# V rows gathered by token and summed on TensorE in four column quarters, h for the U dot products in PSUM

## The reference, cut to what matters

```python
q = (hf @ w_q).astype(f32).reshape(t, PEER_HEADS, 2, PEER_HALF)
...
s1, i1 = lax.top_k(scores[:, :, 0], PEER_TOPK)
s2, i2 = lax.top_k(scores[:, :, 1], PEER_TOPK)
...
idx = (e1 * N_KEYS + e2).reshape(t, PEER_HEADS * PEER_TOPK)
gates = jax.nn.softmax(top_s, axis=-1).reshape(t, PEER_HEADS * PEER_TOPK)
...
def block(args):
    hb, ib, gb = args
    act = jax.nn.gelu(jnp.einsum('td,tkd->tk', hb, u_tab[ib]).astype(f32), approximate=False)
    return jnp.einsum('tk,tkd->td', (gb * act).astype(hb.dtype), v_tab[ib])
```

## Time and profile before

| | us |
|---|---|
| median of three executions | 3935.57 |
| lowest, highest | 3903.57, 3950.37 |
| profiled execution, span from the first to the last instruction | 3815.1 |
| busy in it: TensorE matmul | 2493.9 |
| VectorE (DVE) | 2729.9 |
| ScalarE (ACT) | 552.7 |
| GpSimd (POOL) | 2477.6 |

### The profile page before, as it was taken

The page is one execution under the profiler, slowest core; times in us unless marked ns, Lnnn a source line. Parts: engine busy times, 40 slices in busy tenths (PEclk is TensorE's granted clock), DMA queues, the critical chain, the costliest instruction groups (busy, mean ns, idle before and its releaser), DMA issues. The chain is left out here.

```text
span 3815.1 us, 28982 instructions
## 1 busy us (share of the span) xinstructions
PE 2493.9 (65%) x7042; PEld 1238.9 (32%) x7042; DVE 2729.9 (72%) x5120; ACT 552.7 (14%) x1065; POOL 2477.6 (65%) x2125
## 2 busy tenths in 40 slices
PE   7999863566677667666766666566666667654166
PEld 4444452422243324322433233323332343211022
DVE  3332045989788878887788778787888788867844
ACT  2221010101111111111111111111111111111011
POOL 1100000687777778777787877787778777877776
PEclk9999986788787778788877888788878788877588
DMA  3334400899899999999999899999999999999998
GB/s 100 110 105 149 163 8 14 299 335 372 328 353 365 349 334 334 361 356 334 344 350 359 318 345 353 343 339 342 356 374 345 341 364 376 346 341 391 369 367 323
DMA packets 349585, 1159.17 MB, mean 304 GB/s; under 512 B 41216, under 2 KB 70800, under 8 KB 348432
## 3 DMA queue, kind: packets, MB, share of 16 engines
q0 software_dynamic: 301024, 1094.89, 78.0%
q1 hardware_dynamic: 46256, 58.69, 4.5%
q10 hardware_dynamic: 2176, 4.35, 0.3%
HBM read 1128.37 MB, written 29.43 MB: 303 GB/s over the span
## 5 line engine op out<-in xcount | busy, mean ns | idle before, releaser
L811 PE MATMUL y_psum<-ring,diag 128*128 128x512 f32 x1984 | 1216.2, 751 | 981.1 <-DMA ring<-in_peer_v_dram,at_row 669.6
L1136 DVE CUSTOM_DVE_ANT_0 ring<-ring,h_e 128x1024 f32<-128x1024 f32 x1024 | 1243.9, 1223 | 377.3 <-DMA ring<-in_peer_u_dram,at_row 367.2
L791 POOL DMA_INDIRECT ring<-in_peer_u_dram,at_row x986 | 1182.0, 1199 | 331.5 <-issue 278.9
L791 POOL DMA_INDIRECT ring<-in_peer_v_dram,at_row x704 | 835.3, 1187 | 217.2 <-issue 196.3
L811 PEld LDWEIGHTS y_psum<-ring,diag 128*128 128x128 f32 x1984 | 418.2, 231 | 1677.9 <-issue 878.0
L1158 DVE SCALAR_TENSOR_TENSOR y<-ring,coef,y 128x1024 f32<-128x1024 f32 x528 | 678.9, 1286 | 207.2 <-DMA ring<-in_peer_v_dram,at_tail 116.5
L791 POOL DMA_INDIRECT ring<-in_peer_v_dram,at_tail x320 | 366.0, 1144 | 119.1 <-issue 94.5
L995 ACT ACTIVATE diag<-ident_m,coef 128x128 f32<-128x128 f32 x496 | 190.6, 399 | 1130.1 <-PE y_psum L811 1014.3
L315 PE MATMUL proj<-hn_T,w_blk 128*128 128x512 f32 x640 | 280.0, 596 | 1.3 <-DVE hn_T L444 1.3
L944 PE MATMUL tile_psum<-w_q,arena 128*128 128x512 f32 x512 | 245.1, 641 | 8.8 <-ACT arena L1076 8.8
L775 POOL COPY at_head<-picks 128x10 uint32<-128x10 uint32 x8 | 4.2, 530 | 313.9 <-DVE picks L1377 312.6
...
...
## 6 DMA issues: line engine op xcount, KB each, us to landing
ring<-in_peer_u_dram,at_row POOLq DMA_INDIRECT x986, 6.3
ring<-in_peer_v_dram,at_row POOLq DMA_INDIRECT x704, 6.3
...
ring<-in_peer_v_dram,at_tail POOLq DMA_INDIRECT x320, 6.3
```

The costliest lines, as they stand in the source:

```text
L791: pool.indirect_dma_start(ring[:, j], None, tables[kind], bass.IndirectOffsetOnAxis(ap=at, axis=0)).then_inc(filled[j], 16)
L811: last = nc.tensor.matmul(y_ps[:, half], diag[:, k % 2], ring[:, slot_of(item, e), half * BANK:(half + 1) * BANK], start=(k == 0), stop=(n ...
L1136: nc.vector.tensor_tensor_reduce(out=ring[:, j], in0=ring[:, j], in1=h2_e[:], scale=1.0, scalar=0.0, op0=ALU.mult, op1=ALU.add, accum_out= ...
```

## The change

- A V gather brings, for one token, the V rows of its 128 picks, one per partition. For this the matrix of picks is turned: TensorE turns `top_id`, DVE copies it to `picks_T`, POOL copies that to `at_T`; a gather's offsets are one column of it. U gathers read `picks` itself.
- The sum over a token's picks is then the sum over partitions. TensorE does it with a weight matrix of 128 picks x 32 columns in which only the token's column is not zero. Four tokens, one of each quarter of the tile, form a group: their outputs are the four quarters of partitions of `y_ps`, so a group is 2 halves x 4 quarters of matmuls 128x32 by 128x512. `spread` holds these weight matrices, written by DVE in blocks of four groups (item "E"), each block once the block two before is used.
- No V sum is left on DVE, no diagonal on ScalarE; `PACE`, `split_v`, `GROUP` are gone. Gelu and gate product are done once for all 128 picks behind the last U; `coef` is turned by TensorE into `y_ps` and copied to `coef_T`.
- The order: first the 80 V of the tile before (20 groups), with 64 U mixed in, then 64 U, then gelu, then the first 48 V (12 groups). `MARKS` lays 26 shares over the first part up to "X", 14 up to "G", the rest over the V at the end, which fall beside the top-k.
- h for the U dot products is in PSUM (`h_ps`, two banks). The mixer's PSUM `bank` shrinks from six to four banks: its steps use other banks, the state products of SSD move behind the solve, and `S_gdn_ready` is waited for ahead of the output projection.
- SP waits for `picks_T_ready` instead of `picks_ready` before it loads the next tile's mixer data. `spread` is zeroed once at the start.

The core of the diff (the renumbered banks of the mixer and of ScalarE's copies are left out):

```diff
 
 
 SLOTS = 10
-GROUP = 32
-LAG = 40
-TAIL = PICKS - LAG
-HEAD = SLOTS
-assert LAG % SLOTS == 0
+QUADS = 4
+STEPS = P // QUADS
+BLOCK_STEPS = 4
+BLOCKS_E = STEPS // BLOCK_STEPS
+FRONT_STEPS = 12
+FRONT = FRONT_STEPS * QUADS
+BACK = P - FRONT
+MIXED_U = 64
+PITCH = 33
+assert BACK % SLOTS == 0
 
 
 def expert_sequence():
-    seq, v = [], 0
-    for n in range(PICKS):
-        seq.append(("U", n, 0))
-        while v < min(LAG, (n + 1) * 4 // 3 + 1):
-            seq.append(("V", TAIL + v, 1))
-            v += 1
-        if n >= LAG:
-            seq.append(("V", n - LAG, 0))
-        if n % GROUP == GROUP - 1:
-            seq.append(("G", n // GROUP, 0))
-        if n == 3:
-            seq.append(("C", PICKS // GROUP - 1, 1))
-        if n % GROUP == 5 and n > GROUP:
-            seq.append(("C", n // GROUP - 1, 0))
-        for at, item in ((8, ("K", 0, 0)), (30, ("F", 0, 1)), (33, ("O", 0, 1)), (LAG - 1, ("X", 0, 0))):
-            if n == at:
-                seq.append(item)
+
+
+    seq, n = [], 0
+    back_steps = STEPS - FRONT_STEPS
+    for g in range(back_steps):
+        i = FRONT_STEPS + g
+        seq += [("V", QUADS * i + q, 1) for q in range(QUADS)]
+        if g % BLOCK_STEPS == 1 and i // BLOCK_STEPS + 1 < BLOCKS_E:
+            seq.append(("E", i // BLOCK_STEPS + 1, 1))
+        to = MIXED_U * (g + 1) // back_steps
+        seq += [("U", k, 0) for k in range(n, to)]
+        n = to
+    for k in range(n, P):
+        if k == n + 4:
+            seq.append(("F", 0, 1))
+        if k == n + 7:
+            seq.append(("O", 0, 1))
+        if k == n + 16:
+            seq.append(("X", 0, 0))
+        seq.append(("U", k, 0))
+    seq += [("G", 0, 0), ("C", 0, 0), ("E", 0, 0), ("E", 1, 0)]
+    for i in range(FRONT_STEPS):
+        seq += [("V", QUADS * i + q, 0) for q in range(QUADS)]
+        if i % BLOCK_STEPS == 1 and i >= BLOCK_STEPS:
+            seq.append(("E", i // BLOCK_STEPS + 1, 0))
     return seq
 
...
+    ends = []
+    for (a, at), (b, to) in zip(MARKS, MARKS[1:]):
+        ends += [at + round((to - at) * (n - a) / (b - a)) for n in range(a + 1, b + 1)]
+    return ends
 
 
 SHARE_ENDS = share_ends()
 
-
-def split_v():
-
-    split, owed, at = ([], []), 0.0, 0
-    for end, (_, on_pe) in zip(SHARE_ENDS, PACE):
-        for kind, n, _ in SEQUENCE[at:end]:
-            if kind == "V":
-                owed += on_pe
-                split[owed < 1].append(n)
-                owed -= owed >= 1
-        at = end
-    return [sorted(s) for s in split]
-
-
-PE_PICKS, DVE_PICKS = split_v()
-
 USES = [len(range(j, len(ORDER[FULL]), SLOTS)) for j in range(SLOTS)]
-FEWER = LAG // SLOTS
+FEWER = BACK // SLOTS
 
 
 def scope(nc):
...
         y = sb("y", [P, D])
-        at_row = sb("at_row", [P, PICKS], U32)
-        at_tail = sb("at_tail", [P, LAG], U32)
-        at_head = sb("at_head", [P, HEAD], U32)
+        picks_T = sb("picks_T", [P, P], U32)
+        at_T = sb("at_T", [P, P], U32)
         ring = sb("ring", [P, SLOTS, D])
         dots = sb("dots", [P, PICKS])
         coef = sb("coef", [P, PICKS])
-        diag = sb("diag", [P, 2, P])
+        coef_T = sb("coef_T", [P, P])
+        spread = sb("spread", [P, 2, QUADS, BLOCK_STEPS * PITCH])
...
-        bank = ps("tile_psum", [P, 6, BANK])
+        bank = ps("tile_psum", [P, 4, BANK])
+        h_ps = ps("h_psum", [P, D])
         y_ps = ps("y_psum", [P, 2, BANK])
...
-                        sp.wait_ge(s["picks_ready"], m)
+                        sp.wait_ge(s["picks_T_ready"], m)
                         sp.wait_ge(s["gates_ready"], m)
                     sp.dma_start(tok[:, 0:TOK_B + SSD_G * P], rows(tok_scr, m)[:, 0:TOK_B + SSD_G * P]).then_inc(s["mix_loaded"], 16)
                     sp.dma_start(tok[:, TOK_B + SSD_G * P:], rows(tok_scr, m)[:, TOK_Q:]).then_inc(s["mix_loaded"], 16)
...
-                    nc.gpsimd.tensor_copy(at_tail[:], at_row[:, TAIL:]).then_inc(s["tail_ready"], 1)
-                    pool.wait_ge(s["tail_ready"], e)
-                if mode != LAST:
-
-                    pool.wait_ge(s["picks_ready"], e + 1)
-                    pool.sem_inc(s["held"])
-                    nc.gpsimd.tensor_copy(at_head[:], picks[:, 0:HEAD]).then_inc(s["head_ready"], 1)
-                    pool.wait_ge(s["head_ready"], e + 1)
-                for turn, item in enumerate(gathers(mode)):
+                for item in gathers(mode):
                     kind, n, back = item
                     j = slot_of(item, e)
-                    if turn == SLOTS and mode != LAST:
-
-                        nc.gpsimd.tensor_copy(at_row[:], picks[:]).then_inc(s["at_ready"], 1)
+                    if item == ("U", 0, 0):
+                        pool.wait_ge(s["picks_ready"], e + 1)
+                        pool.sem_inc(s["held"])
+                    if item == ("U", P - 8, 0):
+                        pool.wait_ge(s["picks_T_ready"], e + 1)
+                        pool.sem_inc(s["held"])
+                        nc.gpsimd.tensor_copy(at_T[:], picks_T[:]).then_inc(s["at_ready"], 1)
                         pool.wait_ge(s["at_ready"], e + 1)
-                    if back:
-                        at = at_tail[:, n - TAIL:n - TAIL + 1]
+                        pool.sem_inc(s["held"])
+                    if kind == "U":
+                        at = picks[:, n:n + 1]
                     else:
-                        assert turn >= SLOTS or n < HEAD
-                        at = (at_row if turn >= SLOTS else at_head)[:, n:n + 1]
+                        t = n % QUADS * STEPS + n // QUADS
+                        at = at_T[:, t:t + 1]
                     pool.wait_ge(used[j], turn_of(item, e))
                     pool.sem_inc(s["held"])
                     pool.indirect_dma_start(ring[:, j], None, tables[kind],
...
                     row_of(1, (y_ps[:, 0], y_ps[:, 1])).then_inc(s["final_row_ready"], 1)
-                if kind != "V" or n not in PE_PICKS:
-                    return
-                k = PE_PICKS.index(n)
-                if k == 0 and mode_of(e) != FIRST:
-                    pe.wait_ge(s["out_ready"], e - back)
-                pe.wait_ge(s["diag_ready"], len(PE_PICKS) * (e - back) + k + 1)
-                after_fill(pe, item, e)
-                for half in range(2):
-                    last = nc.tensor.matmul(y_ps[:, half], diag[:, k % 2], ring[:, slot_of(item, e), half * BANK:(half + 1) * BANK],
-                                            start=(k == 0), stop=(n == PE_PICKS[-1]))
-                last.then_inc(used[slot_of(item, e)], 1)
+                if kind == "C":
+                    pe.wait_ge(s["coef_ready"], e + 1)
+                    if mode_of(e) != FIRST:
+                        pe.wait_ge(s["out_ready"], e)
+                    nc.tensor.transpose(y_ps[:, 0, 0:P], coef[:], ident[:]).then_inc(s["coef_turned"], 1)
+                if kind == "V" and n % QUADS == QUADS - 1:
+                    i = n // QUADS
+                    b, at = i // BLOCK_STEPS, i % BLOCK_STEPS * STEPS
+                    if i % BLOCK_STEPS == 0:
+                        pe.wait_ge(s["spread_ready"], BLOCKS_E * (e - back) + b + 1)
+                    four = [("V", QUADS * i + quad, back) for quad in range(QUADS)]
+                    for token in four:
+                        after_fill(pe, token, e)
+                    for half in range(2):
+                        for quad, token in enumerate(four):
+                            j = slot_of(token, e)
+                            last = nc.tensor.matmul(y_ps[quad * STEPS:(quad + 1) * STEPS, half],
+                                                    spread[:, b % 2, quad, at:at + STEPS],
+                                                    ring[:, j, half * BANK:(half + 1) * BANK],
+                                                    start=(i == 0), stop=(i == STEPS - 1))
+                            if half:
+                                last.then_inc(used[j], 1)
 
             def row_of(r, out):
 
...
                 share(last=True)
+                if m is not None:
+                    pe.wait_ge(s["top_id_ready"], 2 * (m + 1))
+                    nc.tensor.transpose(bank[:, 2, 0:P], top_id.rearrange("p h k -> p (h k)"), ident[:]).then_inc(s["picks_turned"], 1)
 
             tile_loop(pe, body)
 
...
-                    nc.scalar.activation(coef[:, group], dots[:, group], ACT.Gelu).then_inc(s["gelu_ready"], 1)
+                    after_use(act, ("U", PICKS - 1, 0), e)
+                    nc.scalar.activation(coef[:], dots[:], ACT.Gelu).then_inc(s["gelu_ready"], 1)
                     nc.scalar.preload_act_table_set(LOG_EXP_SET)
-                if kind == "V" and n in PE_PICKS:
-                    k = PE_PICKS.index(n)
-                    act.wait_ge(s["coef_ready"], PICKS // GROUP * (e - back) + n // GROUP + 1)
-                    if k >= 2:
-                        after_use(act, ("V", PE_PICKS[k - 2], back), e)
```

(51 more changed lines are left out.)

118 lines of the change are left out of this document (51 added, 67 removed).

## The result

| | before, us | changed, us | ratio, 95% interval |
|---|---|---|---|
| the first measurement | 3927.97 | 4157.70 (4 runs, 4144.51 to 4174.15) | 1.060, 1.054 to 1.066 |
| repeated on chip A | 3913.36 | 4162.78 | 1.065, 1.058 to 1.072 |
| repeated on chip B | 3839.30 | 3824.40 | 0.9955, 0.993 to 0.998 |

The prediction was 3842 us, within 3680 to 3990. The first measurement is 6% slower than before: wrong, and on the wrong side. Four chips came up in this study, here A, B, C and D. A came up in the first and in the last group of experiments, the others in one group each, so "chip" here stands for the chip and whatever comes with it. Which one the first measurement had is not recorded; its traces look like A's. The second and third line of the table turned out to be most of the story.

What follows compares the result with a forecast made beforehand. Gathers set the pace, held at 1.54 us each by POOL's issue. From the 3815.1 us span: full tiles -132, tile 0 -20, tile 7 -4, last piece +59, setup +3 give 3721; with the median's 120 above, 3842 us, range 3680 to 3990.

Steps and rivals of the forecast that it cites:

- (b): V matmuls on PE: four quarters run one after another, 7.0 us per group at full clock; 4125 us; chance 15%.
- (c): V gathers by token move slower, 1.72 us each at 305 GB/s; decides from 1.50; 4170 us; chance 8%.
- (d): Tile boundary bubble is 20 us and landing under a full DMA 7 us; no gain left, 3935; chance 5%.
- POOL's port: Gathers on POOL, no longer held by two-SBUF-input DVE instructions, fall from 1.20 to 0.94 us; step 1.24 us.
- DMA floor of 1.31 us: DMA engines at 400 GB/s: least time per gather; the 64 U without V were to run at it.
- V steps on PE: V sums on TensorE: 8 steps per group, 3.9 us at full clock, 5.4 us mixed; 173 us per tile.
- rival (a): V matmuls on PE: four quarters truly at once, DMA sets 1.31 us per gather all over; 3730 us; chance 27%.
- The loop: Ring of ten slots in V-only stretches: two groups take at least 11.3 us, 1.41 us per gather.
- The boundary bubble: Tile's end, SP waiting for picks_T, then mixer loads: 8 us left over per tile, between 0 and 20.
- Tile 0: First tile, 176 gathers instead of 216; first part 192 us at most; 320 us against 340.
- Coefficient chain 5 us: Between last U and first V: gelu, gate product, turn of coef and first spread cost about 5 us.
- Four banks: Mixer in four PSUM banks: costs nothing while gathers set the pace, some 5 us per tile without that cover.

Runs made afterwards that it cites:

- h-from-SBUF run: Changed kernel with the U dots' second operand from SBUF, query weight columns in h's place: 4045.82 us, 1.034 of before on A; 1.049 on D.
- The earlier turn: Changed kernel with TensorE's turn of the picks three V steps earlier: 4111.29 us, 1.053 of before on A; 0.981 on B.

## Why the prediction was wrong, and where it was right

**The step that failed first** is the sentence that the median of 3935.57 lies 120 us above the profile's span of 3815.1 and is left as it is. Three percent between a profile and its own kernel's median is not a constant to add: in the later runs, which list both, an execution's time lies 1.6 to 2.2 us over its span. The span, and the absence of any "remote" wait in that trace, are what B, C and D show (before 3824 to 3839); the median is near what A shows (3913; before was never profiled on A). The rows that I reasoned from and the time that I was asked for came, by this evidence, from different chips, and on A the change costs what no row of before could show: 338 us more than on B (4162.78 for 3824.40), while before costs only 74 more. The sum has no term for engines that are late with nothing to wait for; the runs show 706 and 790 us of such waits. None of my rivals had it. Rivals (b) with 4125 us and (c) with 4170 us lie within 1% of the 4158 measured, and (d) with 3935 us has no gain either, but (b) and (c) got their numbers from mechanisms that are refuted below, and (d) from bubbles: the nearness is luck. What makes the engines late on A stays open.

Measured against B, where the rows apply, the sum said 0.975 of the span and the runs say 0.9955. It goes term by term. Windows of the changed kernel on B:
```profile
672.00:959.00 287.00, 143.71 (x637) 81.73 (x637) 236.22 (x561) 25.73 (x45) 177.40 (x178) 0.70 0.90 331
959.00:1352.00 393.00, 214.65 (x990) 98.18 (x990) 244.49 (x572) 27.38 (x49) 252.12 (x258) 0.70 0.94 351
...
2537.00:2927.00 390.00, 209.67 (x990) 97.06 (x990) 244.39 (x572) 27.37 (x49) 253.15 (x257) 0.71 0.94 353
...
3317.00:3677.00 360.00, 114.05 (x530) 25.24 (x530) 162.03 (x279) 4.52 (x7) 240.06 (x257) 0.57 0.98 373
3677.00:3819.00 142.00, 73.38 (x352) 17.22 (x352) 3.15 (x10) 1.65 (x4) 74.95 (x80) 0.62 0.83 305
```
| | predicted | on B | |
|---|---|---|---|
| tile 0 | 320 | 287 | -33 |
| six full tiles | 373 | 393 (390 to 397) | +120 |
| tile 7 | 357 | 360 | +3 |
| last piece | 133 | 142 | +9 |
| span | 3721 | 3819 | +98 |

- **POOL's port: right.** U gathers 0.95 us, V 1.02, against "near 0.97"; the hold by the compares stays. The step of 1.24 us is the shortest interval seen. The inference of the Trainium skill (SBUF — State Buffer, Who interferes with whom), that a two-input instruction doesn't hold descriptor generation, does not hold for these gathers by the h-from-SBUF run either: same kernel, gathers of 1.14 for 0.95 us, 5.3% slower on D than the changed kernel on B. The gathers read their offsets from SBUF, too, so it may be this reading that is held and not the making of descriptors; no run separates the two.
- **DVE at 245 us a tile: right,** 244.5.
- **DMA floor of 1.31 us: reached once.** Not in the forecast kernel (1.40 us for the U without V), but in the port alone; its tile 7 takes 335 us, which is 256 x 1.31:
```profile
3265.00:3600.00 335.00, 156.71 (x264) 55.18 (x263) 240.64 (x331) 37.39 (x78) 250.90 (x259) 0.73 1.02 404
```
- **V steps on PE: wrong in two terms that nearly cancel.** I took 8 steps of 0.67 us, 5.4 us a group. Timeline of PE, then of POOL, in the last piece on B:
```profile
3756.64 1.92 PE L802 MATMUL y_psum<-ring,spread 128*32 128x512 f32 x16 [1.68 <-DMA ring<-in_peer_v_dram,at_T]
3762.39 3.64 PE L802 MATMUL y_psum<-ring,spread 128*32 128x512 f32 x16 [3.82 <-DMA ring<-in_peer_v_dram,at_T]
```
```profile
3755.75 0.94 POOL L774 DMA_INDIRECT ring<-in_peer_v_dram,at_T  x1 [3.86 <-PE y_psum L802]
3756.99 0.93 POOL L774 DMA_INDIRECT ring<-in_peer_v_dram,at_T  x1 [0.30 <-issue]
...
3767.09 0.94 POOL L774 DMA_INDIRECT ring<-in_peer_v_dram,at_T  x1 [1.72 <-issue]
```
  Sixteen passes span 1.92 us at 2.4 GHz and 3.64 at 1.2, 4 steps of 0.48 and of 0.91: four quarters at once, as rival (a) had it. Its clock was wrong, as mine was: the windows without a mixer, where PE has almost only V steps, were granted 0.57 to 0.62, not 0.8, and the median group of the last piece is 3.5 us. All four slots come free together at its end, and a gather follows 0.8 to 1.1 us later. The loop is 0.8 + 1.24 (the group's fourth token is the second gather of a release) + 5.4 (from that gather's start to PE's) + 3.6 = 11.0 us here and 12.2 in the mean of the piece (8 x 1.52), for the 11.3 that I had: 1.52 us per gather for 1.41. Without half of V's columns the kernel is 4% faster on B, and the step in the last piece falls from 1.52 to 1.34 us. That points to PE's time in this loop as the largest single cost of the V path, but the edit also takes PE's code fetches from 77 to 21, and the two aren't separated.
- **The boundary bubble: in the range, not in the sum.** 8 us taken, 15 to 17 measured on either chip, 8 x 6 = 48 us of the 98. The load of the earlier trace rows (20.8 us there, 17.7 in the median on B) is in it; the first measurement:
```profile
1869.54 0.29 DVE L1393 CAST picks_T<-tile_psum 128x128 uint32<-128x128 f32 x1 [15.44 <-PE tile_psum L975]
...
1873.61 0.51 SPq L742 DMA_DIRECT2D arena<-zgs_scr  x1
...
1889.88 1.22 PE L824 MATMUL tile_psum<-arena 128*128 128x128 f32 x4 [20.45 <-DMA arena<-zgs_scr]
```
  I set POOL's ten slots (13 us) against the whole chain. But the last V step, the turn and 16 us of landing stand in a row; POOL fills its last slot with the gather at 1878.67 and starts again at 1895.47. The earlier turn takes 1.4% off on B. The rest of a tile's +20 us: U without V 90 for 84, front V 81 for 73, the mixed part 2 less than the sum.
- **Tile 0: wrong the other way.** Its 80 U beside the mixer took 138 us for the 192 "at most", so it is 33 us shorter than the sum and hides a part of what the full tiles lose.
- **Coefficient chain 5 us: right on B** (3 to 4 us at V10), 16 to 29 on A.
- **x2's load:** not in the sum; U90 waits 7 to 8 us in every full tile on B, behind DVE's add that waits for it.
- **Four banks "cost nothing", "some 5 us per tile" without cover:** alone they cost some 5 us, on A (2 to 9 by the interval).
- **Rivals (b) and (c): refuted** by the spans above and by landings of 6.3 us for V and 6.4 for U on B. The last piece's 1.52 us per gather lies past (c)'s mark of 1.50, but the ring's loop gives it.

In sum: the port reading carried the change further than I said (0.964 alone), and the new V path gives back some 3.2 of these 3.6 points, 1.4 of it by where the picks are turned. The one comparison is across D and B, each against its own before.

## The version that beats both

The port alone, the kernel before with h in PSUM and the mixer in four banks: 3688.59 us on D, 0.964 of before and, ratio against ratio, 0.968 of the changed kernel on B. On A it is 0.999, and the changed kernel 1.060 to 1.065 there. The changed kernel with the earlier turn is 0.981 on B. The kernels with half of V's columns, 0.956 to 0.959, are left out here: they don't compute the whole sum.
